# The expert weights of a decoder trunk as transfers of two units (2 MB), three for each chunk in place of six

## What is computed

```python
def swiglu(x, w_gate, w_up, w_down):
    return (jax.nn.silu(x @ w_gate) * (x @ w_up)) @ w_down

def moe_swiglu(x, w_router, w_gate, w_up, w_down):
    ...
    for e in range(N_EXPERTS):
        out = out + combine[:, e:e + 1] * swiglu(t, w_gate[e], w_up[e], w_down[e]).astype(jnp.float32)
```

## Time and profile before

| | before |
|---|---|
| median of three runs | 1761.65 us (1760.83 to 1761.86) |
| the profiled execution | 1760.82 us |
| its span, first to last instruction | 1759.1 us |
| TensorE busy | 1723.6 us, 98% of the span |
| VectorE, ScalarE busy | 77%, 63% |
| granted TensorE clock, mean of the span | 0.998 |
| expert transfers | 336 of 1024 KB, median 7.2 to 7.4 us from issue to landing |

### The profile page before, as it was taken

One profiled execution on the slowest core, in us unless ns is written; L12 is line 12 of the kernel. 1 busy time (PEld: TensorE's weight loads), 2 busy tenths in 40 slices (PEclk: granted clock), 3 DMA queues, 4 the chain that ended last, 5 costly groups with the idle time before them and its releaser, 6 DMA issues.

```text
span 1759.1 us, 28116 instructions
## 1 busy us (share of the span) xinstructions
PE 1723.6 (98%) x10872; PEld 1581.7 (90%) x10872; DVE 1356.2 (77%) x1155; ACT 1110.9 (63%) x854; POOL 76.3 (4%) x145
## 2 busy tenths in 40 slices
PE   8999999999999999999999999999999999999997
PEld 7999999999999999999888888888888888888885
DVE  4755676744465666567999989999989999899998
ACT  4544254533445543356777778777777787777775
POOL 0300200000000301100000000000000000000100
PEclk9999999999999999999999999999999999999999
DMA  8635524454534636443999999999999999999994
GB/s 335 229 114 188 182 98 191 144 192 143 193 132 168 220 127 227 149 163 135 360 395 394 392 389 377 391 388 413 397 360 402 392 403 390 361 401 391 412 421 178
DMA packets 75922, 498.63 MB, mean 283 GB/s; under 512 B 11162, under 2 KB 11674, under 8 KB 17968
## 3 DMA queue, kind: packets, MB, share of 16 engines
q1 hardware_dynamic: 68304, 482.38, 70.6%
q0 software_dynamic: 5920, 11.58, 2.0%
q10 hardware_dynamic: 1600, 3.31, 0.7%
HBM read 485.85 MB, written 4.72 MB: 279 GB/s over the span
## 4 chain that ended last, share of the span: by engine, by line
PE 52%; DVE 3%; ACT 1%; issue 1%; DMA 1%; ACTq 0%; DVEq 0%
PE ps L804 11%; PE ps L805 11%; PE ps L806 11%; PE ps L1208 6%; PE ps L1211 5%; PE ps L1210 5%; DVE w_lo L2013 2%; PE ps L1186 1%; ACT w_hi L1337 1%; PE ps L1231 1%; DMA raw<-in_moe_w_up 1%; DVE ag_lo L2330 0%; PE ps L901 0%; PE ps L1009 0%; PE ps L1005 0%
## 5 line engine op out<-in xcount | busy, mean ns | idle before, releaser
L2013 DVE TENSOR_TENSOR w_lo<-raw,w_hi 128x2048 fp32r<-128x2048 f32 x335 | 760.3, 2289 | 72.3 <-ACT w_hi L1337 67.8
L1337 ACT ACTIVATE w_hi<-raw 128x2048 fp32r<-128x2048 f32 x337 | 641.9, 1908 | 154.7 <-PE ps L806 76.4
L487 DVE TENSOR_TENSOR w_lo<-raw,w_hi 128x2048 fp32r<-128x2048 f32 (+2 forms) x126 | 272.4, 2170 | 191.7 <-ACT w_hi L476 190.9
L804 PE MATMUL ps<-rows_hi,w_lo 128*128 128x272 f32 (+1 forms) x1376 | 395.2, 287 | 13.1 <-DVE w_lo L487 8.2
L805 PE MATMUL ps<-rows_lo,w_hi 128*128 128x272 f32 (+1 forms) x1376 | 393.1, 286 | 0.0
L806 PE MATMUL ps<-rows_hi,w_hi 128*128 128x272 f32 (+1 forms) x1376 | 393.0, 286 | 0.0
L804 PE MATMUL ps<-w_hi,xg_lo 128*128 128x512 f32 x896 | 357.2, 399 | 0.4 <-DVE w_lo L2013 0.2
L476 ACT ACTIVATE w_hi<-raw 128x2048 fp32r<-128x2048 f32 (+2 forms) x130 | 234.3, 1807 | 176.5 <-PE ps L806 138.5
L805 PE MATMUL ps<-w_lo,xg_hi 128*128 128x512 f32 x896 | 339.6, 379 | 0.0
L806 PE MATMUL ps<-w_hi,xg_hi 128*128 128x512 f32 x896 | 339.6, 379 | 0.0
L804 PEld LDWEIGHTS ps<-rows_hi,w_lo 128*128 128x128 f32 x1376 | 260.1, 189 | 15.7 <-DVE w_lo L487 8.2
(11 more groups left out here) (351 smaller groups left out, 1826.1 us busy)
## 6 DMA issues: line engine op xcount, KB each, us to landing
raw<-in_dense_units SPq DMA_DIRECT2D x116, 1024.0 KB, 4.9
raw<-in_moe_w_gate SPq DMA_DIRECT2D x112, 1024.0 KB, 7.3
raw<-in_moe_w_up SPq DMA_DIRECT2D x112, 1024.0 KB, 7.4
raw<-in_moe_w_down SPq DMA_DIRECT2D x112, 1024.0 KB, 7.2
raw<-in_dense_units SPq DMA_DIRECT2D x10, 512.0 KB, 4.2
result_rows<-rows POOLq DMA_DIRECT2D x7, 512.0 KB, 8.8
v_tok<-turned_v POOLq DMA_DIRECT2D x48, 64.0 KB, 3.1
srT<-o_tok ACTq DMA_DIRECT2D x6, 272.0 KB, 4.6
```

The lines of the kernel that those rows point to most:

```text
L487: nc.vector.tensor_tensor(w_lo[:, u % HALVES, 0:k * n], raw[:, u % RAW, 0:k * n], w_hi[:, u % HALVES, 0:k * n].bitcast(F32), ALU.subtract) ...
L804: nc.tensor.matmul(dst, l_lo, r_hi, start=start, stop=False)
L1337: return nc.scalar.activation(dst, src, ACT.Copy, **kw)
L2013: tt(w_lo[:, at % HALVES, :], raw[:, at % RAW, :], w_hi[:, at % HALVES, :].bitcast(F32), ALU.subtract).then_inc(lo_ready, 1)
```

## The change

Two units that follow each other (both of a gate, both of an up, or both of a down matrix) come as one transfer of 128 x 2 x 2048 floats into two neighbouring slots of `raw`. The two units lie one behind the other in HBM, so a partition reads two rows of 8 KB that are 1 MB apart. SP waits until the second slot of the two is free, where it used to wait for each slot by itself. Both units are announced by one semaphore, that of the even slot, and ACT waits on it for either unit. The dense units keep their transfers and semaphores.

```diff
-            def load_expert(slot, u, src):
-                sp.wait_ge(lo_ready, u - RAW + 1)
-                sp.dma_start(raw[:, slot, :], src).then_inc(raw_landed[slot], 16)
+            def load_pair(slot, u, src):
+                sp.wait_ge(lo_ready, u + 1 - RAW + 1)
+                sp.dma_start(raw[:, slot:slot + 2, :], src).then_inc(raw_landed[slot], 16)
...
             def chunk_weights(i0, u, e, j):
-                for i, (name, half) in enumerate((("moe_w_gate", 0), ("moe_w_gate", 1), ("moe_w_up", 0), ("moe_w_up", 1))):
-                    load_expert((at + i0 + i) % RAW, u + i, gate_up(e, name, half, j))
+                for i, name in ((0, "moe_w_gate"), (2, "moe_w_up")):
+                    load_pair((at + i0 + i) % RAW, u + i, gate_up(e, name, j))
...
             def down_weights(i0, u, e, j):
-                for i in range(2):
-                    load_expert((at + i0 + i) % RAW, u + i, down(e, j * 2 + i))
+                load_pair((at + i0) % RAW, u, down(e, j * 2))
...
-                act.wait_ge(raw_landed[at % RAW], uses * 16 + 16)
+                act.wait_ge(raw_landed[at % RAW // 2 * 2], uses * 16 + 16)
```

More of the change, by code:

```diff
@@ L687, in _, with gate_up @@
                     move_values(turned_behind[u])
-            def load_expert(slot, u, src):
-                sp.wait_ge(lo_ready, u - RAW + 1)
-                sp.dma_start(raw[:, slot, :], src).then_inc(raw_landed[slot], 16)
-            def gate_up(e, name, half, j):
-                return w[name][bass.ds(e, 1), bass.ds(j, 1), half, :, :].rearrange("e j p n -> p (e j n)")
+            def load_pair(slot, u, src):
+                sp.wait_ge(lo_ready, u + 1 - RAW + 1)
+                sp.dma_start(raw[:, slot:slot + 2, :], src).then_inc(raw_landed[slot], 16)
+            def gate_up(e, name, j):
+                return w[name][bass.ds(e, 1), bass.ds(j, 1), :, :, :].rearrange("e j i p n -> p (e j i) n")
             def down(e, r):
-                return w["moe_w_down"][bass.ds(e, 1), bass.ds(r, 1), :, :].rearrange("e r p n -> p (e r n)")
+                return w["moe_w_down"][bass.ds(e, 1), bass.ds(r, 2), :, :].rearrange("e r p n -> p (e r) n")
             at = NS % RAW
             def chunk_weights(i0, u, e, j):
-                for i, (name, half) in enumerate((("moe_w_gate", 0), ("moe_w_gate", 1), ("moe_w_up", 0), ("moe_w_up", 1))):
-                    load_expert((at + i0 + i) % RAW, u + i, gate_up(e, name, half, j))
+                for i, name in ((0, "moe_w_gate"), (2, "moe_w_up")):
+                    load_pair((at + i0 + i) % RAW, u + i, gate_up(e, name, j))
             def down_weights(i0, u, e, j):
-                for i in range(2):
-                    load_expert((at + i0 + i) % RAW, u + i, down(e, j * 2 + i))
+                load_pair((at + i0) % RAW, u, down(e, j * 2))
             def expert(g, e, seam=False):
@@ L1564, in third_unit @@
                 if q == 0:
-                    act.wait_ge(raw_landed[u % RAW], u // RAW * 16 + 16)
+                    act.wait_ge(raw_landed[u % RAW // 2 * 2], u // RAW * 16 + 16)
                     act.wait_ge(units_used, u - HALVES + 1)
```

## The result

The changed kernel takes 1804.18 us (median of four runs, 1803.61 to 1804.78); the kernel before, run beside it, 1761.76 us (1760.83 to 1762.21). The ratio is 1.0243, 95% interval 1.023 to 1.0255: **42.4 us slower**. The forecast was 1769.5 us, with a range up to 1784.

A forecast was written before the change was run, and what follows sets the result against it. TensorE, busy for 98% of the span, was taken as the bound, with the DMA engines close behind. Gathers 3.4, stores 3.2 and remaining chunks 2 us, 8.6 in all, on 1760.82 gave 1769.5 us; range 1762.0 to 1784.

The forecast's parts named there:

- What is removed: On SP, 168 of 336 issues go, some 0.33 us each, hidden behind waits for DVE; put at nothing.
- The pair lands after 7.3 us: Expert weight transfers: a lone unit's 4.8 us plus 2.46 for one more transfer, in an empty queue.
- the case in which the backlog stays: In the DMA queue, backlog remains as work before the pair, which lands after 9.4 us, just inside the limit.
- the bound of 8.9 from the earlier trace: Upper bound for a pair's landing: a couple of single units in an empty queue, 8.9 us after the first's issue.
- standing backlog of 2.1 us: In the DMA queue, the part of today's 7.2 us median landing that a lone unit and its predecessor leave unexplained.
- The limits of 9.6 to 10.4 us: In the steady chunk, TensorE stops only if a pair takes more than 9.6 (down), 9.7 (gate) or 10.4 us (up).
- The rest of the 56 chunks: Chunks of the expert part apart from gathers and stores: 2 us lost, between nothing and 17 us.
- The gathers: Between 1640 and 1690 us, four gathers read rows back; a pair lands 3.4 us past the limit, counted once.
- The stores: Seven stores of 512 KB each queue 1.2 us of DMA work; 0.45 us each, 3.2 us (0 to 6.3).
- the feed becomes the bound: Rival: in nearly each chunk the gate pair passes 9.7 us; 0.5 us for each of 56, 1789 us; chance 0.10.
- the margins hold: Rival: pairs land under 7.3 us, in time for ACT; only gathers may cost, 1760.8 to 1764.2 us; chance 0.27.
- The signs announced: Right: landing median 7.5 to 9, ACT waits 15 to 60; wrong: waits below 6 us or period above 16.3.

The follow-up runs named there:

- light-down kernel: The changed kernel, with the down pair bringing only the first half of each row (5 MB a chunk in place of 6): 1764.76 us, ratio 1.0017.
- the shorter loop: The changed kernel, with DVE subtracting only the first half of each expert unit: 1761.53 us, ratio 1.0003.
- the 1 MB halves: The changed kernel, with each pair as two transfers of 64 partitions, both waited for: 2371.66 to 2480.41 us in four runs.
- the ring of four: The kernel before, 1 MB transfers with their own semaphores, each unit issued two units later (four ahead of DVE in place of six): 1834.55 us, ratio 1.0422.
- one pair of three: The changed kernel, with only the up couple as a pair, from the second chunk on; gate and down as in the kernel before: 1774.49 us, ratio 1.0065.

## Why the prediction was wrong

The sign, the place and the chain (a landing, then ACT, then DVE, then TensorE) were forecast; the size was five times too small. By the prediction's steps:

- **What is removed: right.** The packets of 8 KB number the same, SP issues 56 transfers of each kind where it issued 112, and no gain from that shows.
- **The pair lands after 7.3 us: wrong by 2.7.** The prediction priced it in an empty queue and kept 9.4 as the case in which the backlog stays. An empty queue gives 7.8 to 8.9: the pairs issued at 777.82, 789.19, 803.67 and 830.52 land after 7.89, 8.63, 7.82 and 8.94, up to the bound of 8.9 from the earlier trace rows. In the stream it is 9.9 at the median (860 to 1680 us). Much of a pair does land near 7.3. The trace has 256 packets of 8 KB for a lone pair, in sixteen chains that run side by side, and sixteen packets of 4 bytes; the semaphore gets sixteen increments, read here as one from each DMA engine. For the gate pair issued at 1131.31 they come, in us after the issue:

```
7.27 7.27 7.29 7.31 7.32 7.34 7.38 7.39 7.39 7.47 8.17 8.38 8.54 9.25 9.87 10.14
```

  A pair is complete when the last of them is, and they are not late together: ten are through by 7.5 us, the last needs 2.7 more. Over all pairs issued between 860 and 1680 us the first increment comes 7.35 us after the issue at the median, the last 9.95. In an empty queue the first came after 6.8 to 7.2 us, the last after 7.8 to 8.9. So what the prediction called a standing backlog of 2.1 us is, for a pair, for the most part the lateness of the slowest engines, and it does not drain.
- **The limits of 9.6 to 10.4 us: too generous.** They held today's issue times fixed. But the issue of a pair waits for DVE's end on the pair a lap earlier, so a late landing also delays the next issue. In the steady loop the limit is 15.99 less 6.7 to 6.9, about 9.1 to 9.3. Put into this loop, the prediction's own 9.4 would have cost 9.4 + 6.9 - 15.99 = 0.3 us a chunk, as much as its upper bound; the later landing adds the other 0.5. The light-down kernel's up pair, at 9.04 on the mean, loses almost nothing; 9.8 loses 42 us.
- **The rest of the 56 chunks, 2 us (0 to 17): the step that failed.** It measured about 40 us, the stores among them (42.4 less the gathers below). It was taken near its lower end "because the latency of the second units already holds most of the backlog", and its upper end relied on "each stop giving the queue time to recover". The first reason fails because the pairs landed after 9.9 us, not after the 7.2 of the second units. The second weighs more: a stop of TensorE delays ACT and DVE, they free the slots later, and the queue gets its next pair later too. In the runs each late landing moves the next issue (the table's 6.91 us, near its least), so no slack is left in which a lap could make up for the one before.
- **The gathers, 3.4 us: of the right size.** From 1680 to 1745 us TensorE idles 4.63 us by the record (905 - 874.85 less 840 - 814.48); at the earlier rate, 25.52 in 840, it would be 2.0, so an estimated 2.7 us are the gathers'. **The stores, 3.2 us**, can't be told apart in a stream that stops in every chunk.
- **The rival "the feed becomes the bound", given 0.10 and 1789 us: nearly what happened.** Against it stood that a chunk of 15.99 us holds 14.8 us of transfer. This weighs the wrong thing: the rate was never short, as 393 GB/s in the shorter loop show. The latency was too long for the ring. The price of 0.5 us a chunk should have been 9.9 + 6.9 - 15.99 = 0.8 us.
- **The rival "the margins hold" falls** with its ground, that the larger transfer lands under 7.3. The Trainium skill (DMA: Bandwidth & Descriptors, 🔬 Anatomy of one DMA — SWDGE (gpsimd) path) has a fit, for transfers issued from GpSimd, of about 2.0 us and the bytes at 436 GB/s, an estimated 6.8 us for a pair. The trace of these transfers, issued from SP, does not agree: 7.8 to 8.9 in an empty queue, 9.9 in the stream.
- **The signs announced.** The prediction called itself wrong at a period above 16.3 us and a wait in nearly every chunk: 17.03 and 117 waits, where 15 to 60 were expected. The landing median of 7.5 to 9 was missed with the landing, the idle of 5 to 15 us with the rest of the chunks.

## What to carry to other kernels

A transfer that fills two slots of a ring is issued when its last slot comes free and, with one semaphore for both, used when its slowest row lands. Before joining transfers, add up the ring's loop (landing as the stream shows it for the slowest engine, the consumers' time up to the release, the next issue) and compare it with the time in which the bound engine uses up what the ring holds: here 9.9 + 6.9 against 15.99 us. A stall in such a loop is paid on every lap, because the stall also delays the next issue; bandwidth to spare doesn't recover it.

## What the runs showed of the hardware

- **Transfers over 64 partitions each run at about half the rate**: 221 GB/s at a DMA share of 1.01, where the kernel before moves 390 at 0.98; the 1 MB halves land after 18.5 to 20.3 us at the median. The Trainium skill (SBUF — State Buffer, Door 1: The DMA port swizzle (why `[64,N]` ≈ `[32,N]`)) says that partitions 0 to 63 lie behind eight of the sixteen ports; the trace agrees in the rate, and no run here shows the ports themselves.
- **The sixteen increments of a 2 MB pair come 2.4 us apart at the median, first to last, and up to 4.2** in the busy stream (7.27 to 10.14 in the pair above). In an empty queue it is 0.8 to 1.4 us for three of four pairs (the one issued at 777.82: 6.84 to 7.89), and 2.1 for the fourth, where a single increment is late (7.84, then 8.94).
- **A stop of TensorE can be followed by the lower clock**: after the longest stop of the change's expert part, 2.15 us, the granted clock is 0.50 for some 3.4 us and matmuls start 0.43 us apart in place of 0.21.
- **The DMA share tells little about the bytes**: between 840 and 1700 us a share of 0.96 went with 362 GB/s in the ring of four and with 386 in one pair of three.
